# Where the constants lie in SBUF: a two-layer decoder trunk with float32 split in two

## What is computed

```python
for layer in range(2):
    y = rmsnorm(h, norm_g[layer, 0])
    y = even_mixer(y, ...) if layer % 2 == 0 else odd_mixer(y, ...)   # attention, in and out projections
    h = h + rmsnorm(y, norm_g[layer, 1])
    y = conv_ffn(rmsnorm(h, norm_g[layer, 2]), ...)
    h = h + rmsnorm(y, norm_g[layer, 3])

def conv_ffn(h, w_up, conv_w, conv_b, w_down):      # w_up 1024 x 5632, w_down 2816 x 1024
    u = h @ w_up
    c = causal depthwise convolution of u, width 3, plus bias
    gate, val = split(c, 2)
    return (gelu(gate) * val) @ w_down
```

## Time and profile before

| | |
|---|---|
| median of 3 runs | 675.29 us (674.56 to 675.3) |
| the profiled execution's own time | 675.03 us |
| its span, first to last instruction | 673.2 us |
| TensorE matmuls, busy | 656.9 us, 98% |
| TensorE weight loads, busy | 548.1 us, 81% |
| VectorE, busy | 459.7 us, 68% |
| ScalarE, busy | 381.6 us, 57% |
| GpSimd, busy | 156.8 us, 23% |

### The profile page before, as it was taken

The page is one execution under the profiler, slowest core; times in us unless marked ns, Lnnn a source line. Parts: engine busy times, 40 slices in busy tenths (PEclk is TensorE's granted clock), DMA queues, the critical chain, the costliest instruction groups (busy, mean ns, idle before and its releaser), DMA issues.

```text
span 673.2 us, 10262 instructions
## 1 busy us (share of the span) xinstructions
PE 656.9 (98%) x3732; PEld 548.1 (81%) x3732; DVE 459.7 (68%) x621; ACT 381.6 (57%) x547; POOL 156.8 (23%) x123
## 2 busy tenths in 40 slices
PE   7999999899999999999999999999999999999996
PEld 5888877577788888888887999777788888888885
DVE  5597777785777878876457645576777878786532
ACT  6646444775665757575345533575467676667320
POOL 0321310000034343432001000490123434344000
PEclk9999999999999999999999999999999999999999
DMA  8976633005254545455652664303354353644601
GB/s 306 407 253 248 245 126 126 1 2 188 76 237 174 200 165 208 163 212 226 221 197 107 250 226 150 126 1 138 119 211 189 136 238 139 233 135 185 245 0 62
DMA packets 18651, 115.61 MB, mean 172 GB/s; under 512 B 2591, under 2 KB 3133, under 8 KB 5693
## 3 DMA queue, kind: packets, MB, share of 16 engines
q1 hardware_dynamic: 17469, 111.52, 44.2%
q10 hardware_dynamic: 1152, 3.67, 1.5%
HBM read 114.14 MB, written 1.05 MB: 171 GB/s over the span
## 4 chain that ended last, share of the span: by engine, by line
PE 89%; DVE 3%; ACT 2%; issue 2%; DMA 1%; POOL 1%; SPq 0%; DVEq 0%; POOLq 0%; ACTq 0%
PE ps L1715 22%; PE ps L1272 13%; PE ps L1274 13%; PE ps L1273 13%; PE ps L1717 11%; PE ps L1314 4%; DMA raw<-in_weights 1%; PE ps L1494 1%; PE ps L1614 1%; PE ps L1766 1%; PE ps L1755 1%; PE ps L1267 1%; PE ps L1472 1%; POOL rstd L1181 1%; PE ps L1540 1%
## 5 line engine op out<-in xcount | busy, mean ns | idle before, releaser
L700 DVE TENSOR_TENSOR wlo<-raw,whi 128x2048 fp32r<-128x2048 f32 x99 | 225.8, 2313 | 66.0 <-ACT whi L360 66.0
L360 ACT CAST whi<-raw 128x2048 fp32r<-128x2048 f32 x99 | 186.2, 1919 | 72.7 <-PE ps L1274 65.8
L1715 PE MATMUL ps<-xpair,whi 128*128 128x512 f32 x640 | 226.4, 399 | 0.0
L1717 PE MATMUL ps<-xpair,wlo 128*128 128x256 f32 x640 | 179.8, 281 | 0.0
L1715 PEld LDWEIGHTS ps<-xpair,whi 128*128 128x128 f32 x640 | 120.3, 188 | 29.9
L1717 PEld LDWEIGHTS ps<-xpair,wlo 128*128 128x128 f32 x640 | 120.9, 189 | 0.0
L1227 POOL TENSOR_TENSOR hidf<-act_g,conv 128x512 f32<-128x512 f32 x22 | 73.9, 3357 | 83.9 <-ACT act_g L604 83.9
L1272 PE MATMUL ps<-whi,hid_hi 128*128 128x512 f32 x176 | 69.4, 394 | 0.0
L1274 PE MATMUL ps<-whi,hid_lo 128*128 128x512 f32 x176 | 69.0, 392 | 0.0
L1272 PE MATMUL ps<-whi,xpair 128*128 128x512 f32 x168 | 67.5, 402 | 1.0 <-DVE pcm L932 0.8
L1273 PE MATMUL ps<-wlo,hid_hi 128*128 128x512 f32 x176 | 68.3, 388 | 0.0
(11 more groups left out here) (193 smaller groups left out, 969.9 us busy)
## 6 DMA issues: line engine op xcount, KB each, us to landing
raw<-in_weights SPq DMA_DIRECT2D x101, 1024.0 KB, 4.9
c_gpost<-in_gpost ACTq DMA_DIRECT2D x4, 512.0 KB, 4.9
raw<-in_weights SPq DMA_DIRECT2D x3, 512.0 KB, 9.1
c_gpre<-in_gpre ACTq DMA_DIRECT2D x3, 512.0 KB, 4.2
h<-in_x SPq DMA_DIRECT2D x2, 512.0 KB, 5.7
out<-h SPq DMA_DIRECT2D x4, 256.0 KB, 2.0
raw<-in_weights SPq DMA_DIRECT2D x2, 256.0 KB, 5.7
t<-in_masks SPq DMA_DIRECT2D x1, 512.0 KB, 12.5
```

Of the source, the lines that this page charges most:

```text
L360: act.copy(whi[:, slot, :], raw[:, slot, :]).then_inc(hi_done, 1)
L700: dve.tensor_tensor(wlo[:, slot, :], raw[:, slot, :], whi[:, slot, :].bitcast(F32), ALU.subtract).then_inc(lo_done, 1)
L1715: pe.matmul(ps[:, b0 + m, :], whi[:, slot, cols], xpair[:, kt].rearrange("p a c -> p (a c)"), start=kt == 0, stop=kt == KT - 1, skip_group ...
L1717: ins = pe.matmul(ps[:, b0 + m, 0:SEQ], wlo[:, slot, cols], xhi[:, kt, :], start=False, stop=kt == KT - 1, skip_group_check=True)
```

## The change

The constants and small tensors, c_gpre to mhalf, are put at the upper end of SBUF, growing downwards, instead of behind wlo. What is declared behind them, hid_hi and hid_lo among it, moves down by their 19,648 bytes and starts directly behind wlo. h, xn, xpair, raw, whi and wlo stay. No instruction, loop or semaphore is touched.

```diff
-        c_gpre = sb("c_gpre", [P, D])
-        c_gpost = sb("c_gpost", [P, D])
-        c_conv = sb("c_conv", [P, 2 * UP_CHUNKS * 4 * 4])
...
-        wg_parts = sb("wg_parts", [P, KT, 2 * CPAD], F32R)
+
+        def top(name, shape, dt=F32):
+            return ctx.enter_context(nc.sbuf_tensor(name, shape, dt, side="right"))
+
+        c_gpre = top("c_gpre", [P, D])
+        c_gpost = top("c_gpost", [P, D])
+        c_conv = top("c_conv", [P, 2 * UP_CHUNKS * 4 * 4])
+        c_rope = top("c_rope", [P, 2, 2, TT, HD])
+        c_ropec = top("c_ropec", [2 * NC, 2, HD])
+        c_cmask = top("c_cmask", [P, 2, TT, NC])
+        c_mask = top("c_mask", [P, NG + 1, SEQ], BF16)
+        c_identf = top("c_identf", [P, P])
+        c_identb = top("c_identb", [P, P], BF16)
+        c_tri = top("c_tri", [P, 2, P])
+
+        wg_parts = top("wg_parts", [P, KT, 2 * CPAD], F32R)
```

More of the change, by code:

```diff
@@ L94, in build @@
         wlo = sb("wlo", [P, RING, UNIT], F32R)
-        c_gpre = sb("c_gpre", [P, D])
-        c_gpost = sb("c_gpost", [P, D])
-        c_conv = sb("c_conv", [P, 2 * UP_CHUNKS * 4 * 4])
[L98 to L104, removed]
-        wg_parts = sb("wg_parts", [P, KT, 2 * CPAD], F32R)
-        tri_r = wg_parts[:].rearrange("p k n -> p (k n)")[:, 0:2 * P].rearrange("p (a c) -> p a c", a=2)
[L109 to L116, removed]
+        def top(name, shape, dt=F32):
[11 more added lines that the diff above has]
+        wg_parts = top("wg_parts", [P, KT, 2 * CPAD], F32R)
+        tri_r = wg_parts[:].rearrange("p k n -> p (k n)")[:, 0:2 * P].rearrange("p (a c) -> p a c", a=2)
+        c_w2 = top("c_w2", [P, 2, 2, HD])
+        c_pe2 = top("c_pe2", [P, 2, CKT])
+        meanh = top("meanh", [P, 2, TT, 2])
+        ms = top("ms", [P, 2, TT])
+        rstd = top("rstd", [P, 2, TT])
+        rstdh = top("rstdh", [P, TT])
+        c_gcol = top("c_gcol", [P, KT])
+        mhalf = top("mhalf", [P, 1])
         a = ctx.enter_context(ExitStack())
```

## The result

The changed kernel takes 671.83 us (median of 6 executions, 669.68 to 672.15) against 675.29 before (674.56 to 677.43): ratio 0.9934, 95% interval 0.9918 to 0.995. The profiled execution took 672.15 us with a span of 670.4.

What follows compares the result with a forecast made beforehand. It took TensorE, busy 98% of the span, as the bound, paced by matmul-to-matmul distance. The hidden pair's -0.89 us, all else 0, took the median from 675.29 to 674.4 us, range 673.4 to 675.7.

Steps and rivals of the forecast that it cites:

- Forecast 0.89 us on the path: Down projections: 504 matmuls on the path gain 1.77 ns each from the hidden pair's move, 0.89 us.
- the bound of 1.00: Down projections: upper bound of the gain, 1.98 ns per matmul from the faster xpair run, 1.00 us.
- the two xpair runs: Two unbroken 47-matmul runs with stationary xpair, together 227.2 ns a matmul, taken as the hidden pair's new pace.
- Rival B: Down projections: nothing changes, the difference comes from hi/lo or tile spacing that stays; 675.3 us, chance 0.21.
- The step that failed: Up, input and output projections: operands keep their addresses, so no cost and no gain was counted.
- The place that was taken at nothing: Transposes, compression, gate and layer 1 sums change distance: taken as 0, bound 0.9 us either way.
- D: Down projections slower, suffering like the up projection at the same place: 3.4 us slower, 678.7 us, chance 0.06.
- C: Transposes, sums and products gain too, or the three lines fall below 389 ns: 1.8 us at most, 673.5, chance 0.13.

Runs made afterwards that it cites:

- c1: The changed kernel, unedited, profiled a second time; 673.28 us, ratio 0.9957 to the kernel before.
- e1: Kernel before with constants left low and 320 unused bytes behind them, putting the hidden pair at the weights' place within 512; 674.57 us, ratio 0.9983.
- e2: Changed kernel with 192 unused bytes behind wlo, so the hidden pair is again 192 bytes off the weights' place; 674.33 us, ratio 0.9976.
- f3: Kernel before with 64 pad elements (256 bytes) behind the constants, hidden pair 256 bytes off the weights' place; 674.09 us, ratio 0.998.
- e3: Kernel before with only the identity c_identf moved to the upper end, at its changed-kernel place within 512; 672.75 us, ratio 0.9964.
- e5: Kernel before with the last transpose of each token tile issued twice ahead of both up projections; 674.26 us, ratio 0.9984.
- e4: Changed kernel with 96 unused bytes at the upper end, putting the identity back at its old place within 512; 674.47 us, ratio 0.9985.
- g1: Kernel before with h to wlo 64 bytes further and the hidden pair at distance 0 from the weights; 673.95 us, ratio 0.9983.
- e6: Kernel before with the two matmuls of each up projection pair in the other order; 674.54 us, ratio 0.9982.
- f2: Kernel before with 256 unused bytes between whi and wlo; 676.11 us, ratio 0.9999.
- g4: Changed kernel with the last transpose of each token tile issued twice ahead of both up projections, second set of executions; 670.15 us, ratio 0.9925.
- f1: Kernel before with 320 unused bytes ahead of the hidden pair, identity moved high, layer 1's last transpose per token tile issued twice; 670.76 us, ratio 0.9922.
- g2: Kernel before with the hidden pair 128 bytes off the weights' place within 512; 676.86 us, ratio 1.0027.

## Why the prediction was wrong

**Right: the down projections.** Forecast 389 ns in all three lines and 59.7 us from first start to last; measured 389, 59.66 and 59.64. Forecast 0.89 us on the path; measured 1.12 over both, of which the 24 matmuls at the end of layer 0 (24 x 2.1 ns = 0.05) lie under other work: in the changed kernel the chain that ended last goes over to ScalarE at 350.49, and the last of the 24 starts at 355.50. That leaves 1.07, just over the bound of 1.00, because the pair's new pace is 226.8 ns (59.66/263) and not the 227.2 of the two xpair runs. Where the up projections stay slow, the forecast comes true almost to the number: c1's profiled execution, at full clock, took 674.26 us against 674.4. Rival B, that hi and lo being 22,528 bytes apart makes the difference, is refuted by e1, where the pair keeps its layout and only its place changes. What B leaned on, the 388 ns of line 1273, tells nothing: in e2, with the pair again 192 off, the three lines have medians of 393, 394 and 390 where the kernel before has 394, 388 and 392, and the down projection takes the same 60.20 us. The starts are what counts. The reason given was half right: the distance counts (59.65 us at 0 in e1, 60.20 at 192 in e2), but it need not be 0 within 512: 256 off takes 59.67 too (f3).

**The step that failed:** "So every up projection and every input and output projection sees the same addresses as before: no cost, no gain for lines 1715, 1717". The addresses are indeed the same, and input and output projections are unchanged. But the up projection's pace does not depend on its own operands' addresses alone. It has a slow and a fast pattern, 2.12 us a layer apart, and the identity's place, in transposes that are issued ahead of the loop (in layer 0 of the kernel before the last four start from 183.50 on, the loop at 183.92), helps to choose: with the identity alone moved, layer 0 took 111.03 us (e3). In the profiled execution 4.24 us are this. The median's gain beyond the forecast, 3.46 against 0.9, is mostly this too: three of the six totals are 671.8 at full clock, which by the sizes is one fast layer of two (2.1 us) and the hidden pair (1.1 us). The size is partly chance. In the second set the same change had a ratio of 0.9957, not 0.9934.

**The place that was taken at nothing.** The prediction did see that the identity moves, priced the move within the transposes alone (at most 0.9 us for all such matmuls) and took 0. Its arithmetic there is wrong as well. Packed downwards from the upper end the tensors come to lie in the reverse order: c_identf moves 96 bytes on within 512, not 128, and so lies 224 from xn; wg_parts comes to lie 32 bytes short of the weights' place, not at it; and the mask and the bf16 identity do not keep their distance but go from 0 to 256 apart.

**The same error in the rivals.** D took up the very number that mattered, 7 ns per pair more in the up projection than the same sizes take elsewhere, and laid it to places that the change would not touch, as a danger for the down projections. It was a gain of up to 640 x 6.6 ns = 4.2 us. That all operands of the up projection lay at distance 0 and it still paid should have said that something else than distance was at work. C held that other matmuls might gain, in the transposes themselves; these took 273 ns before and after.

**The profile misled by being the same twice.** 113.14 us in both layers looked like a property of the stage. It was one of two values.

## What to carry to other kernels

Where TensorE runs without a gap, compare start to start the same matmul sizes in different stages: 353.6 ns a pair in one and 347 in the others (227 for 512 columns, and 120 for 256: 45.95 us over the 384 of layer 1's input projection) is 4 us in this kernel, and an unexplained difference is a place to look, not a constant. Where stationary and streaming operands meet without a gap, try them at the same place within 256 bytes: that was the fastest of the places tried here (59.64 to 59.68 us a down projection against 60.19 to 61.36), and it took 320 unused bytes of a partition (e1). Profile a result more than once before laying a change of 0.3% to a cause: here one program had totals of 669.7, 671.8 and 674.3 us at full clock.

## What the runs showed of the hardware that was not expected

- A back-to-back stream of matmuls of 512 and 256 columns had two steady paces here, 353.6 and 346.9 ns a pair. Each of the 36 profiled layers took 113.1 or 111.0 us for its 320 pairs; none was in between. Which it is changed with two more transposes ahead of the stream in each layer (e5) and with the place of the identity, which those transposes read (e3, e4).
- With the identity 224 bytes from xn (within 256) the pattern can differ between executions of one program (the changed kernel: both layers fast, both slow); with 128 it was slow in every profiled execution of eight kernels whose loop and entry were those of the kernel before, though three of the 111 totals of the kernel before, and one of g1's ten (672.00), are low enough for one fast layer.
- A matmul's pace in the down projection (512 columns) changed here with the distance between what streams and the stationary tile: 226.8 to 226.9 ns at 0 and 226.9 at 256, 228.9 at 192, 232.4 at 128, 233.3 at 32.
- The same wait of TensorE is followed by a granted clock of 0.50 in some executions and not in others. All 18 profiled executions have a wait of 0.77 us at 95 to 96 us and one of 1.38 us at 431 to 435 us. The clock fell behind the first in five of them (the changed kernel, e1, e6, f2, g4) and behind the second in five (the changed kernel, e4, e6, f1, g2), about 1.6 us each time.

Open: why the identity's place reaches into the loop. No run shows it. The starts at the entry agree within about 0.01 us between the patterns up to the third pair, and the fourth pair starts 1.119 to 1.129 us behind the first in the fast layers and 1.132 to 1.147 in the slow ones (all profiled layers but those of e6). Other distances of the identity, and other amounts of work ahead of the loop, were not tried.
